# Gate and up weights read in 4 MB transfers, 32 KB per partition, into two neighbouring places of a weight ring

## The chip, the cores and the metric

The kernel runs on one core of a Trainium2 chip. The metric is device microseconds of one execution, median over several. The kernel is written engine by engine: TensorE (PE), VectorE (DVE), ScalarE (ACT), GpSimd (POOL) and SyncE (SP) each have their own program, and they meet only in semaphores. SP and POOL both issue DMA transfers; the 16 DMA engines of the core carry them all.

## The reference

One layer of a hybrid decoder on 320 tokens (256 of a prompt, 64 sampled), everything in float32. Two recurrent branches are merged, projected by `w_o` and added to the input; then a mixture of 32 experts follows, four per token. Cut to what matters:

```python
logits = x2d @ w_router + b_router
top_v, top_e = lax.top_k(logits, TOP_K)            # 4 of 32
gates = softmax(top_v)
def expert(x, e):                                  # d_model 1024, d_ff 1024
    gu = x @ w_gate_up[e] + b_gate_up[e]           # 1024 x 2048: 8 MB
    gate, up = minimum(gu[:, :D_FF], 7), clip(gu[:, D_FF:], -7, 7)
    return ((up + 1) * gate * sigmoid(1.702 * gate)) @ w_down[e] + b_down[e]   # 1024 x 1024: 4 MB
y = rms(x + sum over the four experts of gate * expert(x, e)) * norm_f_w
```

The experts' weights are 32 x 12 MB, 402.7 million bytes, and each byte is used once.

## The kernel before

**Up to the experts.** The mixing part takes about 370 us of the run; its weight panels go through slots 0 to 4 of the ring below (`MIX = 5`), and the four pieces of `w_o` into slots 8 to 11. Then come the product with `w_o`, the norm, the router and the placing of tokens. On PE this is one row of instructions; ahead of the transposes at L1095 (`bgu`) PE waits for `s_late`, a semaphore that six loads issued by POOL raise (L577 to L582: the norm weights broadcast to all partitions) together with two earlier ones. The expert stage begins on PE at the first `gate_up`.

**The ring.** `ring` has 16 slots of 8 KB per partition. For the experts two neighbouring slots make a place (`chunk(p)`, 16 KB per partition, 2 MB), so there are eight places. An expert has six chunks of 2 MB: `c` = 0 to 3 are rows of `w_gate_up`, 256 each (a partition holds two whole neighbouring rows, one run of 16 KB in memory), and `c` = 4, 5 are 512 rows of `w_down` each (four rows of 4 KB per partition, again one run of 16 KB). Chunk `c` of expert `e` has the number `g = 6 e + c` and goes into place `g % 8`. Each place has two semaphores: `e_full[p]`, which the transfer raises by 16, and `e_free[p]`, which PE raises by one when it has read the place.

**SP** first issues eight chunks by hand (`load(g, e)`): 3, 1, 2, 0 as ring slots come free from the mixing panels, 6 and 7 (the first two of expert 1), and, behind the last product with `w_o` (`wo11`), 4 and 5. From `g = 8` on it goes through the chunks in order: wait for the place, issue. SP stands still at each such wait, so transfers are issued in the order of `g`.

**PE** handles two experts in a round (`pair`). `gate_up` reads the four gate/up chunks in order, waiting for each; both halves of the gate and up rows of the 64 token slots come out in two PSUM banks. Then DVE and ACT make the activation while PE does the scatter of the expert before, or the gather of the ones to come, and `down_chunk` reads the two down chunks. The loop runs 8 times over four experts.

Of the kernel before, what the change touches and what calls it, by code (L numbers as in the profile page):

```python
# [51 lines left out]
PIECES = RING // 2  # L52
# [71 lines left out]
def build(nc, x_prompt, x_sample, state_gdn, state_gdn_conv, state_gla, norm1_w, w_in, conv_w, a_log, dt_bias,  # L124
# [3 lines left out]
    with ExitStack() as ctx:  # L128
# [275 lines left out]

        def expert_chunk(e, c):

            w, r, i = (w_gate_up, 256 * c, 2) if c < GU else (w_down, 512 * (c - GU), 4)
            rows_of = w[0][bass.ds(e, 1), r:r + 128 * i, :]
            return rows_of.rearrange("e (p i) n -> p (e i n)", i=i)

# [6 lines left out]
        def piece(e, c):  # L417

            g = CHUNKS * e + c
            return g % PIECES, g // PIECES  # L420

        block = ctx.enter_context(nc.Block())


        @block.sync
        def _(sp):
            for s in range(2):
                sp.dma_start(x_tm[:, s, :], x_prompt[0, 128 * s:128 * s + 128, :]).then_inc(s_x[s], 16)
            sp.dma_start(x_tm[0:64, 2, :], x_sample.rearrange("b t d -> (b t) d")).then_inc(s_x[2], 16)
            sp.dma_start(rows[0:8, :], norm1_w[0].rearrange("(k p) -> k p", p=128)).then_inc(s_rows, 16)  # L430
            sp.dma_start(rows[8:56, :], conv_w[0].rearrange("j (t p) -> (j t) p", p=128)).then_inc(s_rows, 16)
            sp.dma_start(rows[56:57, :], gdn_norm_w).then_inc(s_rows, 16)
            sp.dma_start(rows[57:58, :], gla_norm_w).then_inc(s_rows, 16)
            sp.dma_start(rows[58:60, :], gla_gk_b[0].rearrange("(k p) -> k p", p=128)).then_inc(s_rows, 16)
            sp.dma_start(rows[60:68, :], norm2_w[0].rearrange("(k p) -> k p", p=128)).then_inc(s_rows, 16)
            sp.dma_start(cst_rows, state_gdn_conv[0].rearrange("b w c -> (b w) c")).then_inc(s_cst, 16)
            for i in range(MIX):
                n = panels[i].shape[1]
                sp.dma_start(slot(i).rearrange("p (k n) -> p k n", k=n), panels[i]).then_inc(wfull[i], 16)
                if i == 0:  # L440
                    sp.dma_start(w_small[:, :, 0:8], win(C_AB, 8)).then_inc(s_small, 16)
                    sp.dma_start(w_small[:, :, 8:24], win(C_LR, 16)).then_inc(s_small, 16)
                    sp.dma_start(gk_up[:, :], gla_gk_up[0]).then_inc(s_small, 16)
                    sp.dma_start(hb[:, 0:4], dt_bias.to_broadcast([128, 4])).then_inc(s_misc, 16)
                    sp.dma_start(hb[:, 4:8], a_log.to_broadcast([128, 4])).then_inc(s_misc, 16)
            sp.dma_start(Sg[:, :, :], state_gdn[0].rearrange("b h d e -> d (b h) e")).then_inc(s_state, 16)
            sp.dma_start(Sl[:, :, :], state_gla[0].rearrange("b h d e -> (b h d) e")
                         .rearrange("(n p) e -> p n e", p=128)).then_inc(s_state, 16)
            sp.dma_start(wr[:, :, :], w_router[0].rearrange("(k p) e -> p k e", p=128)).then_inc(s_misc, 16)
            sp.dma_start(brt[:, :], b_router.to_broadcast([128, EXPERTS])).then_inc(s_misc, 16)  # L450
            for i in range(MIX, MIX_PANELS):

                full(sp, last_use[i - MIX])
                n = panels[i].shape[1]
                sp.dma_start(slot(i % MIX).rearrange("p (k n) -> p k n", k=n), panels[i]).then_inc(wfull[i % MIX], 16)
            sp.wait_ge(o_ready, 2)
            full(sp, f"gss{HEADS - 1}1")
            for k in range(WO):
                src = w_o[0][256 * k:256 * k + 256, :].rearrange("(k p) n -> p k n", p=128)
                sp.dma_start(wo_slot(k).rearrange("p (k n) -> p k n", k=2), src).then_inc(wfull[MIX + k], 16)  # L460

            def load(g, e):
                p = g % PIECES
                sp.dma_start(chunk(p), expert_chunk(e, g % CHUNKS)).then_inc(e_full[p], 16)

            load(3, 0)
            for i in range(MIX_PANELS - MIX, MIX_PANELS):
                full(sp, last_use[i])
                if i % MIX in (3, 4, 0):
                    load({3: 1, 4: 2, 0: 0}[i % MIX], 0)  # L470
            sp.wait_ge(out_sem, 16 * 6)
            load(6, 1)
            load(7, 1)
            full(sp, "wo11")
            load(4, 0)
            load(5, 0)
            for g in range(PIECES, 4 * CHUNKS):
                sp.wait_ge(e_free[g % PIECES], g // PIECES)
                load(g, g // CHUNKS)

            def load_quad(i, first):
                for g in range(4 * CHUNKS):
                    sp.wait_ge(e_free[g % PIECES], i * USES + g // PIECES)
                    load(g, first + g // CHUNKS)

            with sp.Fori(1, QUADS) as i:
                load_quad(i, i * 4)
            sp.wait_ge(cnt_ready, 1)
            its = sp.value_load(nit[0:1, 0:1], min_val=QUADS, max_val=QUADS * ROUNDS)
            with sp.If(its > QUADS):  # L490
                with sp.Fori(QUADS, its) as i:
                    load_quad(i, (i % QUADS) * 4)
            sp.wait_ge(fin_dve, 1)
            sp.dma_start(y_prompt[0, 0:128, :], x_tm[:, 0, :]).then_inc(y_out, 16)
            sp.wait_ge(fin_dve, 2)
            for f in range(2):
                sp.dma_start(y_sample.rearrange("b t d -> (b t) d")[:, 512 * f:512 * f + 512],
                             xs[64 * f:64 * f + 64, :]).then_inc(y_out, 16)
            sp.wait_ge(fin_dve, 3)
            sp.dma_start(y_prompt[0, 128:256, :], x_tm[:, 1, :]).then_inc(y_out, 16)  # L500

            sp.wait_ge(out_sem, 16 * 6)
            sp.wait_ge(y_out, 64)
# [3 lines left out]
        def _(pool):  # L507
# [27 lines left out]
            for g in range(2, 4):  # L535
# [14 lines left out]
            step(pool.memset(gb_rows[0:64], 0.0), consts)  # L550


            pool.dma_start(n2p[:, :].rearrange("p (k i) -> p k i", i=2), norm2_w[0].rearrange("(k p i) -> p k i", p=128, i=2)
                           ).then_inc(s_n2p, 16)
            freed(pool, "tail2")
            pool.dma_start(conv_p[0, 0], tail_tm[0:3, :]).then_inc(out_sem, 16)
# [34 lines left out]
        def _(pe):  # L591
# [458 lines left out]
            def first_tokens(s, f):  # L1050

                o = p3(bank[f], 4, 2 * SLOTS)
                pe.wait_ge(first_ready, TILE_ORDER.index(s) + 1)
                for k in range(4):
                    c = 256 * (k // 2) + k % 2
                    if s < 2:
                        lhs, rhs = x_tm[:, s, 512 * f + c:512 * f + c + 255:2], Psel[:, s, :]
                    else:
                        u = slice(64 * f, 64 * f + 64)
                        lhs, rhs = xs[u, c:c + 255:2], Psel[u, 2, :]  # L1060
                    mm = pe.matmul(o[:, k, :], lhs, rhs, start=(s == TILE_ORDER[0] and k == 0),
                                   stop=(s == TILE_ORDER[-1]), skip_group_check=True)
                return mm
# [10 lines left out]
            def turn_tokens(f):  # L1074

                o = p3(bank[f], 4, 2 * SLOTS)
                for k in range(4):
                    c = 512 * f + 256 * (k // 2) + k % 2
                    mm = pe.transpose(o[:, k, :], xr[:, c:c + 255:2], ident[:, :])  # L1079
                mm.then_inc(xt_full[f], 1)  # L1080

            o = take("wo2")
# [74 lines left out]
            def gate_up(x, e, i):  # L1157

                for k in range(KD):
                    p, u = piece(e, k // 2)  # L1160
                    if k % 2 == 0:
                        pe.wait_ge(e_full[p], i * (16 * USES) + (16 * u + 16))
                    for q in range(2):
                        mm = halves(bank[PRE[q]], xTe[:, k, SLOTS * x:SLOTS * x + SLOTS],
                                    chunk(p)[:, 2048 * (k % 2) + FF * q:2048 * (k % 2) + FF * q + FF], k == 0, k == KD - 1)
                    if k % 2:
                        mm.then_inc(e_free[p], 1)
# [7 lines left out]
            def down_chunk(x, e, i, c):  # L1175

                p, u = piece(e, c)
                pe.wait_ge(e_full[p], i * (16 * USES) + (16 * u + 16))
                for j in range(4):
                    mm = halves(bank[DN[x]], hm[x][:, j, c - GU, :], chunk(p)[:, D * j:D * j + D], c == GU and j == 0,  # L1180
                                c == CHUNKS - 1 and j == 3)
                mm.then_inc(e_free[p], 1)
# [854 lines left out]
```

## Time and profile before

| | |
|---|---|
| median of 3 runs | 1367.11 us (1364.9 to 1369.3) |
| the profiled execution | 1367.33 us |
| its span, first to last instruction | 1365.6 us |
| PE busy | 1290.9 us, 95% of the span |
| read from memory | 442.30 MB, 328 GB/s over the span |
| experts' stage | from 434 us on; 425 to 430 GB/s from 444 us to 1331 us |

The span and the time of the profiled execution differ by 1.7 us. PE's busy share counts instructions that overlap and can't be read as a share of its peak; a better reading is where it waits and for what. GB/s is what all 16 DMA engines moved. A transfer appears in the trace as packets on an engine; here one packet is one partition's run, 16 KB for the experts' weights.

### The profile page before, as it was taken

How to read it: one execution, taken by the hardware profiler on the slowest of the kernel's cores; microseconds unless marked ns; L12 is line 12 of the kernel's file. 1: busy time of each engine (PE TensorE's matmuls, PEld its weight loads, DVE VectorE, ACT ScalarE, POOL GpSimd, SP SyncE). 2: the span in 40 equal slices, each digit the busy share in tenths (PEclk: the TensorE clock that was granted, in tenths of full speed). 3: DMA queues.
4: the chain of work that ended last, by engine and by line, in shares of the span. 5: the costliest groups of instructions: out<-in, count | busy, mean ns of one | idle time of the engine just before them, and what ended most of it. 6: DMA issues, size and time to landing. Idle time of an engine off the chain costs nothing.

```text
span 1365.6 us, 15570 instructions
## 1 busy us (share of the span) xinstructions
PE 1290.9 (95%) x5889; PEld 613.5 (45%) x5889; DVE 437.3 (32%) x814; ACT 287.0 (21%) x527; POOL 33.6 (2%) x73
## 2 busy tenths in 40 slices
PE   7999989989989999999999999999999999999996
PEld 5777678746645333333333333333333333333332
DVE  3536565274115231223212322122321212322123
ACT  2375552130022011111110211101111010111103
POOL 6000000001000000000000000000000000000000
PEclk9999989999999999999999999999999999999999
DMA  9622300226584999999999999999999999999993
GB/s 270 182 76 84 94 31 2 62 70 229 221 327 179 425 427 428 427 429 429 429 429 428 429 429 429 429 428 429 428 429 429 428 429 428 429 430 427 429 428 155
DMA packets 61885, 447.76 MB, mean 328 GB/s; under 512 B 7637, under 2 KB 30249, under 8 KB 37276
## 3 DMA queue, kind: packets, MB, share of 16 engines
q1 hardware_dynamic: 59836, 440.34, 78.4%
q0 software_dynamic: 2016, 6.99, 1.5%
q8 instruction: 20, 0.33, 0.1%
q14 instruction: 13, 0.11, 0.0%
HBM read 442.30 MB, written 5.02 MB: 328 GB/s over the span
## 4 chain that ended last, share of the span: by engine, by line
PE 65%; DMA 26%; DVE 6%; ACT 1%; issue 1%; POOL 0%; DVEq 0%; SPq 0%; ACTq 0%
PE bank L668 31%; DMA ring<-in_w_gate_up_dram 24%; PE bank L617 14%; PE bank L1072 5%; DMA xbuf<-in_norm_f_w_dram 2%; PE bank L1079 2%; PE bank L1172 1%; PE bank L871 1%; PE bank L682 1%; PE bank L1006 1%; PE bank L883 1%; PE bank L879 1%; PE bank L1151 1%; DVE qkgb L1987 1%; PE bank L1144 0%
## 5 line engine op out<-in xcount | busy, mean ns | idle before, releaser
L668 PE MATMUL bank<-ring,zgb 128*64 128x512 f32 x2560 | 562.0, 594 | 36.1 <-DMA ring<-in_w_gate_up_dram 27.7
L668 PEld LDWEIGHTS bank<-ring,zgb 128*64 128x64 f32 x2560 | 181.4, 137 | 413.4 <-issue 344.0
L1978 DVE COPY zgb<-bank 128x512 f32<-128x512 f32 x32 | 22.1, 692 | 614.5 <-PE bank L668 614.5
L617 PE MATMUL bank<-hTb,ring 128*128 128x320 f32 x640 | 179.2, 438 | 1.3 <-DVE hTb L1574 1.3
L617 PEld LDWEIGHTS bank<-hTb,ring 128*128 128x128 f32 x640 | 121.7, 192 | 53.7 <-issue 4.6
L668 PE MATMUL bank<-ring,oABb 128*64 128x512 f32 x512 | 116.9, 598 | 0.0
L1504 ACT COPY zgb<-bank 128x512 f32<-128x512 f32 x32 | 18.7, 586 | 419.4 <-PE bank L668 419.4
L1514 ACT COPY hTb<-bank 64x512 f32<-64x512 f32 x64 | 37.1, 579 | 197.6 <-PE bank L668 196.6
L1072 PE MATMUL bank<-h2b,oABb 128*128 128x512 f32 (+1 forms) x192 | 78.3, 609 | 0.0
L1151 PE MATMUL bank<-hTb 128*128 128x512 f32 x136 | 68.2, 606 | 0.0
L1951 DVE TENSOR_TENSOR xbuf<-xbuf,bank 128x512 f32<-128x512 f32 x85 | 58.4, 687 | 20.6 <-PE bank L668 11.2
L668 PEld LDWEIGHTS bank<-ring,oABb 128*64 128x64 f32 x512 | 33.9, 136 | 58.7 <-issue 54.8
L1172 PEld LDWEIGHTS bank<-ident,zgb 128*128 128x128 f32 x256 | 39.1, 204 | 35.1 <-ACT zgb L1504 19.9
L1987 DVE TENSOR_TENSOR qkgb<-bank,masks 128x512 f32<-128x512 f32 x64 | 44.3, 692 | 27.8 <-PE bank L1172 19.4
L1172 PE MATMUL bank<-ident,zgb 128*128 128x128 f32 x256 | 42.3, 288 | 0.0
L617 PE MATMUL bank<-oABb,ring 128*128 128x320 f32 x128 | 38.9, 460 | 2.0 <-DVE oABb L1825 2.0
L1072 PEld LDWEIGHTS bank<-h2b,oABb 128*128 128x128 f32 (+1 forms) x192 | 27.0, 190 | 28.3 <-issue 28.3
L617 PEld LDWEIGHTS bank<-oABb,ring 128*128 128x128 f32 x128 | 25.6, 203 | 16.4 <-issue 4.9
L1151 PEld LDWEIGHTS bank<-hTb 128*128 128x128 f32 x136 | 22.3, 193 | 22.9 <-issue 22.9
L1491 ACT COPY h2b<-bank 128x512 f32<-128x512 f32 x32 | 18.7, 585 | 61.3 <-PE bank L1072 61.3
L1495 ACT COPY zgb<-bank 128x512 f32<-128x512 f32 x32 | 18.7, 585 | 59.1 <-PE bank L1079 58.4
L1508 ACT ACTIVATE qkgb<-qkgb 128x512 f32<-128x512 f32 x32 | 20.2, 630 | 42.7 <-DVE qkgb L1989 42.2
(384 smaller groups left out, 952.4 us busy)
## 6 DMA issues: line engine op xcount, KB each, us to landing
ring<-in_w_gate_up_dram SPq DMA_DIRECT2D x128, 2048.0 KB, 30.5
ring<-in_w_down_dram SPq DMA_DIRECT2D x64, 2048.0 KB, 34.9
ring<-in_w_in_dram SPq DMA_DIRECT2D x22, 1024.0 KB, 5.4
ring<-in_w_o_dram SPq DMA_DIRECT2D x4, 1024.0 KB, 12.5
ring<-in_w_up_a_dram SPq DMA_DIRECT2D x2, 1024.0 KB, 5.0
ring<-in_w_up_b_dram SPq DMA_DIRECT2D x2, 1024.0 KB, 5.0
out_dram<-ring POOLq DMA_DIRECT2D x1, 2048.0 KB, 14.2
xbuf<-in_x_prompt_dram SPq DMA_DIRECT2D x2, 512.0 KB, 4.0
```

Source lines behind the costliest of these rows:

```text
L617: mm = pe.matmul(o[0:m, 0:TOK], w[:, k, c0:c0 + m], rhs[:, k, :], start=(k == 0), stop=(k == kk - 1))
L668: mm = pe.matmul(o[64 * f:64 * f + 64, 0:width], lhs, w[f] if isinstance(w, list) else w[:, width * f:width * f + width], start=start, sto ...
L1072: return pe.matmul(o[:, :], lhs, rhs, start=(s == TILE_ORDER[0]), stop=(s == TILE_ORDER[-1]))
L1079: mm = pe.transpose(o[:, k, :], xr[:, c:c + 255:2], ident[:, :])
L1151: mm = pe.matmul(bank[SC[j]][:, :], GTs[:, TILE_0[s]:TILE_0[s] + 128], y_sl[:, 512 * f:512 * f + 512], start=True, stop=True)
L1172: mm = pe.transpose(bank[FMB[q]][:, 128 * j:128 * j + 128], pre[:, q, j:512:4], ident[:, :])
L1491: link(nc.scalar.copy(xr[:, 512 * f:512 * f + 512], bank[7 - f][:, :]), xr_done, done)
L1508: link(A(sbuf_[:, :, :, :], gbuf[:, :, :, :], ACT.Sigmoid, scale=ALPHA), sg_ready, n * 2 + (x + 1))
L1514: ins = nc.scalar.copy(y_sl[SLOTS * x:SLOTS * x + SLOTS, 512 * f:512 * f + 512], bank[DN[x]][64 * f:64 * f + 64, :])
L1951: link(TTo(v, v, bank[SC[j]][:, :], ALU.add), acc_done, n * 5 + i)
L1978: link(V.tensor_copy(pre[:, 1, :], bank[PRE[1]][:, :]), pre_done[1], n * 2 + (x + 1))
L1987: inner(TTo(dst[:, :, :, :], src, bias, ALU.add))
```

## The change

A transfer of gate/up weights now takes 512 rows, four per partition: a run of 32 KB, 4 MB in all, into two neighbouring places. `load` is called for chunks 1 and 3 of an expert after both places are free (chunks 0 and 2 only wait) and issues for the pair; it raises `e_full` of the first place alone. PE waits once per pair (`landed` works out the count), and still gives the two places back one by one. Since a partition holds rows 4p to 4p+3 now instead of 2p and 2p+1, the gathered tokens are taken with a step of 4 instead of 2 (`first_tokens`, `turn_tokens`), and so is the norm weight `n2p`. The down chunks are as they were. In the hand-written start, the separate loads of chunks 3 and 1 are gone, and that of chunk 7.

```diff
-            w, r, i = (w_gate_up, 256 * c, 2) if c < GU else (w_down, 512 * (c - GU), 4)
+            w, r, i = (w_gate_up, 256 * c, 4) if c < GU else (w_down, 512 * (c - GU), 4)
...
+        def landed(eng, e, i, c):
+
+            g = CHUNKS * e + c
+            starts = [q for q in range(4 * CHUNKS) if q % PIECES == g % PIECES and q % CHUNKS not in (1, 3)]
+            eng.wait_ge(e_full[g % PIECES], i * (16 * len(starts)) + 16 * (starts.index(g) + 1))
...
-                p = g % PIECES
-                sp.dma_start(chunk(p), expert_chunk(e, g % CHUNKS)).then_inc(e_full[p], 16)
-
-            load(3, 0)
+                p, c = g % PIECES, g % CHUNKS
+                n = 8192 if c < GU else 4096
+                sp.dma_start(ring[:, 4096 * p:4096 * p + n], expert_chunk(e, c)).then_inc(e_full[p], 16)
+
             for i in range(MIX_PANELS - MIX, MIX_PANELS):
                 full(sp, last_use[i])
-                if i % MIX in (3, 4, 0):
-                    load({3: 1, 4: 2, 0: 0}[i % MIX], 0)
+                if i % MIX in (4, 0):
+                    load({4: 2, 0: 0}[i % MIX], 0)
             sp.wait_ge(out_sem, 16 * 6)
             load(6, 1)
-            load(7, 1)
             full(sp, "wo11")
             load(4, 0)
             load(5, 0)
             for g in range(PIECES, 4 * CHUNKS):
                 sp.wait_ge(e_free[g % PIECES], g // PIECES)
-                load(g, g // CHUNKS)
+                if g % CHUNKS not in (0, 2):
+                    load(g - (g % CHUNKS < GU), g // CHUNKS)
...
-                    c = 512 * f + 256 * (k // 2) + k % 2
-                    mm = pe.transpose(o[:, k, :], xr[:, c:c + 255:2], ident[:, :])
+                    mm = pe.transpose(o[:, k, :], xr[:, 512 * f + k:512 * f + 512:4], ident[:, :])
...
                     p, u = piece(e, k // 2)
-                    if k % 2 == 0:
-                        pe.wait_ge(e_full[p], i * (16 * USES) + (16 * u + 16))
+                    if k % 4 == 0:
+                        landed(pe, e, i, k // 2)
```

SP's program just ahead of the experts' stage, before: `pfull` are the semaphores of the mixing part's last products, `outputs` that of the stored states, `piece_free` that of a place.

```order
L460 DMA ring<-in_w_o_dram 128x2x1024 x3
L464 DMA ring<-in_w_gate_up_dram 128x4096
L464 DMA ring<-in_w_gate_up_dram 128x4096 [waits pfull6,pfull5,pfull4]
L464 DMA ring<-in_w_gate_up_dram 128x4096 [waits pfull3]
L464 DMA ring<-in_w_gate_up_dram 128x4096 [waits pfull4]
L464 DMA ring<-in_w_gate_up_dram 128x4096 [waits outputs]
L464 DMA ring<-in_w_gate_up_dram 128x4096
L464 DMA ring<-in_w_down_dram 128x4096 [waits pfull7]
L464 DMA ring<-in_w_down_dram 128x4096
L464 DMA ring<-in_w_gate_up_dram 128x4096 [waits piece_free0]
L464 DMA ring<-in_w_gate_up_dram 128x4096 [waits piece_free1]
```

The same place of SP's program now (`w_o` stands at L466, `load` at L471):

```order
L466 DMA ring<-in_w_o_dram 128x2x1024 x3
L471 DMA ring<-in_w_gate_up_dram 128x8192 [waits pfull6,pfull3,pfull5,pfull4]
L471 DMA ring<-in_w_gate_up_dram 128x8192 [waits pfull4]
L471 DMA ring<-in_w_gate_up_dram 128x8192 [waits outputs]
L471 DMA ring<-in_w_down_dram 128x4096 [waits pfull7]
L471 DMA ring<-in_w_down_dram 128x4096
L471 DMA ring<-in_w_gate_up_dram 128x8192 [waits piece_free1,piece_free0]
```

The transfer that followed `w_o` without a wait (chunk 3) is no longer there; its 2 MB now come with the first transfer behind the mixing part's last product, and the first refill of the ring waits for two places instead of one.

PE's program at the first `gate_up` of a round, before (`piece_full` is raised by a transfer):

```order
L668 MATMUL bank<-ring,zgb 64x512 [waits piece_full0]
L668 MATMUL bank<-ring,zgb 64x512 x7
L668 MATMUL bank<-ring,zgb 64x512 [waits piece_full1]
L668 MATMUL bank<-ring,zgb 64x512 x7
L668 MATMUL bank<-ring,zgb 64x512 [waits piece_full2]
L668 MATMUL bank<-ring,zgb 64x512 x7
L668 MATMUL bank<-ring,zgb 64x512 [waits piece_full3]
```

And now (the matmuls stand at L675):

```order
L675 MATMUL bank<-ring,zgb 64x512 [waits piece_full0]
L675 MATMUL bank<-ring,zgb 64x512 x15
L675 MATMUL bank<-ring,zgb 64x512 [waits piece_full2]
L675 MATMUL bank<-ring,zgb 64x512 x15
```

Four waits of PE have become two, each for 4 MB. (In this listing one row is a pair of the instructions that the profile counts, so x16 in a profile row is one place.)

## Rows read from the trace of the kernel before

**Rows 1.** The page: GB/s in 40 slices of the span, 34.1 us each.

```profile
GB/s 270 182 76 84 94 31 2 62 70 229 221 327 179 425 427 428 427 429 429 429 429 428 429 429 429 429 428 429 428 429 429 428 429 428 429 430 427 429 428 155
```

**Rows 2.** Chain that ended last, 1270 to 1366: start us, us, what.

```profile
1299.63 33.40 DMA ring<-in_w_gate_up_dram
```

**Rows 3.** Timeline of PE, 1297 to 1355: start, us, instructions [idle before <- releaser].

```profile
1328.18 3.65 PE L668 MATMUL bank<-ring,zgb 128*64 128x512 f32 x16 [0.82 <-DMA ring<-in_w_gate_up_dram]
1333.08 3.65 PE L668 MATMUL bank<-ring,zgb 128*64 128x512 f32 x16 [1.24 <-DMA ring<-in_w_gate_up_dram]
```

**Rows 4.** Chain that ended last, 420 to 700: the same place of two rounds.

```profile
509.29 20.82 PE bank L668 x96
...
564.47 20.82 PE bank L668 x96
```

**Rows 5.** Landing, issue to last byte, of ring transfers issued at 373.8, 437.7, 1307.5.

```profile
DMA to landing us min/median/max: 32.4/32.4/32.4
...
DMA to landing us min/median/max: 7.8/7.8/7.8
...
DMA to landing us min/median/max: 35.2/35.2/35.2
```

**Rows 6.** Chain that ended last, 371 to 434.5.

```profile
374.54 25.25 DMA xbuf<-in_norm_f_w_dram
...
399.83 1.13 PE bank L1095 x4
```

**Rows 7.** Timeline of PE, 430 to 462.

```profile
433.99 13.95 PE L668 MATMUL bank<-ring,zgb 128*64 128x512 f32 x64 [0.91 <-DVE zgb L1934]
```

**Rows 8.** Timeline of SP's issues, 330 to 480: first issue, length of the row, transfers.

```profile
340.54 33.81 SPq L464 DMA_DIRECT2D ring<-in_w_gate_up_dram  x6
...
437.68 3.76 SPq L464 DMA_DIRECT2D ring<-in_w_gate_up_dram  x2
...
457.69 10.63 SPq L464 DMA_DIRECT2D ring<-in_w_gate_up_dram  x4
```

**Rows 9.** DMA queues, 345 to 351: packets, MB, share of 16 engines.

```profile
q1 hardware_dynamic: 652, 2.49, 102.5%
```

**Rows 10.** DMA queues, 600 to 1300 (q1 is SP's, q0 POOL's).

```profile
q1 hardware_dynamic: 20597, 299.98, 100.7%
```

**Rows 11.** DMA queues, 371 to 407.

```profile
q1 hardware_dynamic: 720, 10.49, 75.9%
q0 software_dynamic: 480, 1.57, 11.3%
```

**Rows 12.** DMA queues, 371 to 376.

```profile
q1 hardware_dynamic: 65, 1.06, 63.9%
```

**Rows 13.** DMA queues, 376 to 389.

```profile
q1 hardware_dynamic: 302, 4.42, 81.2%
q0 software_dynamic: 287, 1.05, 20.2%
```

**Rows 14.** DMA queues, 389 to 399.8.

```profile
q1 hardware_dynamic: 228, 3.23, 86.9%
q0 software_dynamic: 193, 0.52, 13.4%
```

**Rows 15.** DMA queues, 323 to 333.

```profile
q0 software_dynamic: 729, 2.92, 76.4%
q1 hardware_dynamic: 788, 0.79, 25.8%
```

**Rows 16.** Instructions of lines 1079 and 1172: duration ns min/median/max, first and last start.

```profile
L1079 PE MATMUL bank<-ident,h2b x128: 281/283/385, 480.8 to 1347.5; 128*128 128x128 f32 x128
...
L1172 PE MATMUL bank<-ident,zgb x256: 272/284/387, 448.8 to 1339.5; 128*128 128x128 f32 x128
```

**Rows 17.** Timeline of PE, 300 to 312.

```profile
304.31 1.13 PE L980 MATMUL bank<-ring,xbuf 32*128 32x512 f32 x4 [2.36 <-DVE ring L1803]
```

**Rows 18.** Busy time by engine in one stretch, then PEclk, DMA share, GB/s.

```profile
305.80:309.20 3.40, 3.40 (x8) 1.51 (x5) 3.19 (x7) 0.00 (x0) 0.00 (x0) 0.50 0.01 2
```

More of the change, by code:

```diff
@@ L483, in load_quad @@
                     sp.wait_ge(e_free[g % PIECES], i * USES + g // PIECES)
-                    load(g, first + g // CHUNKS)
+                    if g % CHUNKS not in (0, 2):
+                        load(g - (g % CHUNKS < GU), first + g // CHUNKS)
             with sp.Fori(1, QUADS) as i:
@@ L550, in _ @@
             step(pool.memset(gb_rows[0:64], 0.0), consts)
-            pool.dma_start(n2p[:, :].rearrange("p (k i) -> p k i", i=2), norm2_w[0].rearrange("(k p i) -> p k i", p=128, i=2)
+            pool.dma_start(n2p[:, :].rearrange("p (k i) -> p k i", i=4), norm2_w[0].rearrange("(k p i) -> p k i", p=128, i=4)
                            ).then_inc(s_n2p, 16)
@@ L1056, in first_tokens @@
                     if s < 2:
-                        lhs, rhs = x_tm[:, s, 512 * f + c:512 * f + c + 255:2], Psel[:, s, :]
+                        lhs, rhs = x_tm[:, s, 512 * f + k:512 * f + 512:4], Psel[:, s, :]
                     else:
                         u = slice(64 * f, 64 * f + 64)
-                        lhs, rhs = xs[u, c:c + 255:2], Psel[u, 2, :]
+                        lhs, rhs = xs[u, k:512:4], Psel[u, 2, :]
                     mm = pe.matmul(o[:, k, :], lhs, rhs, start=(s == TILE_ORDER[0] and k == 0),
@@ L1177, in down_chunk @@
                 p, u = piece(e, c)
-                pe.wait_ge(e_full[p], i * (16 * USES) + (16 * u + 16))
+                landed(pe, e, i, c)
                 for j in range(4):
```

## The prediction

> **What bounds the kernel now.** I read first what the DMA moves over the span. From slice 14 on, that is from 444 us to 1331 us, it moves 425 to 430 GB/s without a gap, and ahead of that far less [rows 1]. So there are two parts: a stretch of 900 us in which the expert weights stream, and what comes before it. Then the chain of waits: its last long piece is a ring transfer that was issued at 1299.6 us and landed 33.4 us later [rows 2], and PE starts on it at once, after waits of 0.8 to 1.2 us [rows 3]. From the first refill of the ring, issued at 437.7 and landed 7.8 us later, to the last, issued at 1307.5 and landed after 35.2 us [rows 5], 183 further places land in 1342.7 - 445.5 = 897.2 us, 4.90 us each. A transfer that lands after 33 us has thus stood behind six others: the queue is full. PE would be a little faster than this. Early on, while it still lives on places filled ahead, two experts take it 564.47 - 509.29 = 55.18 us [rows 4]; their twelve places take the DMA 12 x 4.90 = 58.8 us. PE has 3.6 us to spare per two experts, and the stream is the bound. Its start matters as much as its rate: the stream can't begin before PE gives back a first place, at 437.7 us, one place after PE's first `gate_up` at 433.99 [rows 7, 8]. And what sets 433.99? The chain there goes through a load of POOL's, 25.25 us long, the last of the norm weights; PE stands at L1095 until it has landed and starts again at 399.83 [rows 6].
>
> **The change, part by part.** The sum is made against the profiled execution, 1367.33 us, 0.2 us above the median of the runs shown.
>
> *Longer packets.* Between 345 and 351 us SP's queue moves 4 KB packets: 2.49 MB are 608 of them in 102.5% of 16 x 6 us, 161.8 ns each [rows 9]. In the stream, 299.98 MB are 18309 packets of 16 KB in 100.7% of 16 x 700 us, 616.0 ns each [rows 10]. The twelve KB between them cost 37.85 ns each, so 10.4 ns of each packet don't depend on its length. The ring brings 122 gate/up places after the start, 61 pairs; a pair has 8 packets per engine fewer. 61 x 8 x 10.4 ns = **-5.1 us**. It is nothing if a run of 32 KB goes as two packets.
>
> *First refill.* The first transfer into the ring now needs two places back. PE gives them back 3.43 us apart (two issues of SP take 3.76 us, the last of them 0.33) [rows 8]. The stream starts **+3.4 us** later.
>
> *A seam.* The next pair, chunks 0 and 1 of expert 2, goes at 461.1 instead of 457.7 [rows 8]. What is ahead of it: the first pair, issued at 441.1, would land at 441.1 + 7.8 + 4.9 = 453.8, two down chunks at 463.6. A transfer into an idle queue lands 2.9 us later than its 4.9 us of data; this one is issued 2.5 us before the queue runs dry: **+0.4 us**. Later pairs come earlier against the queue, since PE gains 3.6 us per two experts.
>
> *Pairs given back late.* In the stream every pair is issued 3.4 us after its first place is free. That costs nothing, for the queue holds six transfers ahead [rows 2]; without that cover it would be 61 x 3.4 = 209 us. PE's wait for 4 MB instead of 2 is hidden too, in the 3.6 us that PE has to spare, but not at the end.
>
> *The last pair.* Chunks 2 and 3 of expert 31 land at the same distance from the end of the stream as chunk 3 did, but PE had read chunk 2 by then [rows 3]. Now it reads both afterwards: **+3.4 us**, and everything behind (activation, down, scatter, norm, output) moves with it.
>
> *The norm loads.* This is the largest term, and it lies before the stream. Chunk 3 was issued at 340.54 [rows 8], in idle time, long before POOL's loads. Now its 2 MB stand with the others behind the mixing part, beside the six loads for which PE waits at L1095. How do the two queues share an engine? From 323 to 333 us POOL's queue moves 2.92 MB in packets of 4 KB, 713 of them, and SP's 0.79 MB in packets of 1 KB, 771 [rows 15]. From 376 to 389 us POOL's moves 1.05 MB, 256 packets, and SP's 4.42 MB, now in packets of 16 KB, 270 [rows 13]. Bytes stand once 4:1 and once 1:4, packets both times 1:1. So an engine takes one packet from each queue in turn, whatever its size, and a packet of POOL's will wait for 32 KB instead of 16. Per engine POOL has 384 / 16 = 24 packets and SP had 640 / 16 = 40 [rows 11]; now SP has 12.6 MB, 24 packets of 32 KB, of which two are gone when POOL's first packet comes, at 376 (65 small ones, 4 per engine, until then [rows 12]). The first 16 turns took 13.0 us [rows 13] and get 16 x 0.61 = 9.8 us longer. The last eight took 10.8 us, with 3.23 MB = 12.3 of SP's packets per engine [rows 14]: 12.3 x 0.616 + 8 x 0.16 = 8.9 us and 1.9 us of pauses. Now SP has only 22 - 16 = 6 left: 6 x 1.22 + 8 x 0.16 + 1.9 = 10.5 us. Together **+9.5 us**, the norm weights land at about 409.3. PE's row behind L1095 is nearly without gaps up to 433.99, so the expert stage moves by the whole of it. Bounds: nothing, if POOL's turn doesn't get longer; and 11.3 us, when POOL's last packet comes behind all of SP's (SP's last transfer landed at 373.8 + 32.4 = 406.2 [rows 5], with 2 MB more at 411.1).
>
> The Trainium skill, page "DMA: Bandwidth & Descriptors", section "Queues, rings and completion order", also has an engine go round its queues packet by packet, but says that a packet is typically 9 to 17 descriptors long, where the trace shows single runs alternate. By that rule SP's 24 runs would pass in two or three turns and POOL's loads would end last: that is the 11.3 us, and the sum below would be 13.4 instead of 11.6.
>
> *The rest.* A step of 4 instead of 2 in the operands costs nothing: transposes with a step of 2 take 283 ns, with 4 they take 284 [rows 16].
>
> Sum: -5.1 + 3.4 + 0.4 + 3.4 + 9.5 = +11.6 us, 1367.3 + 11.6 = **1379 us**.
>
> **The rivals.**
> *A run of 32 KB goes as two packets of 16 KB.* Then POOL's turns stay as they are and the saving is nothing: 3.4 + 0.4 + 3.4 = +7.2, 1374.5 us. The rows have no packet above 16 KB that could exclude it.
> *POOL's loads aren't held up, the saving holds.* +7.2 - 5.1 = +2.1, 1369.4 us, no measurable change. It needs an engine that shares by bytes, which rows 13 and 15 both speak against.
> *Faster: a price per transfer goes with the transfers.* In the ring 61 transfers fewer are issued. If each seam between transfers cost the stream something, that is saved; it decides from (11.6 + 4.1) / 61 = 0.26 us per seam, and 0.3 us would give 1367.3 + 11.6 - 18.3 = 1360.6 us. Against it: a place lands every 4.90 us, and its 8 packets per engine alone take 8 x 0.616 = 4.93, so no time is left for a seam.
> The same page of the Trainium skill, section "Anatomy of one DMA — SWDGE (gpsimd) path", fits 2.0 us of fixed cost per transfer besides its bytes. Were that paid at every seam, 61 x 2.0 = 122 us would go and the time be about 1257; the 4.90 us per place show it hidden behind the queue.
> *Slower still: PE's clock falls in the longer waits.* PE's waits, up to 1.2 us each now, gather into one per expert, the longer of them over 2 us. At 304.3 us PE had idled 2.36 us, and from 305.8 to 309.2 the granted clock was 0.50, the lower of its two levels, 1.2 of 2.4 GHz [rows 17, 18]; that costs half of 3.4 us, 1.7 us. Twice per two experts makes 55.2 + 3.4 = 58.6 us, still just the stream's 58.8, so only the tail pays, +1.7, 1380.7 us; if PE becomes the bound in part, up to 1386.
>
> **How the numbers follow.** Chances: the sum as it stands 0.64, two packets 0.11, the clock 0.07, POOL unhindered 0.10, faster 0.08. About 0.3%, 4.1 us, is what a measurement of this kernel tells from no change; so the first three are slower, 0.82 together, the fourth is no change and the fifth faster. The range must leave out no more than 0.2: it reaches from 1371, which leaves out the last two, to 1386, which takes in the upper bound of the norm loads (1380.8) and the clock; the lower one is the fourth case.
>
> **What would show it.** Right: PE's wait at L1095 ends near 409 instead of 399.8, its first `gate_up` starts near 443.5; the first refill is issued 7.1 us after that; packets of 32 KB near 1222 ns; the stream from first issue to last landing near 900 us instead of 905; the last wait of PE is followed by 32 matmuls of L675 instead of 16. Wrong: POOL's loads landing by 400, which takes off 9.5 us; packets that are no cheaper, or dearer, per byte (1% of the stream is 9 us); gaps in the stream, where a pair waits for its second place with an empty queue.

## The result, and the profile after

| | before | changed |
|---|---|---|
| median | 1366.71 us (1364.9 to 1369.3, 4 runs) | 1388.09 us (1384.02 to 1393.19, 4 runs) |
| profiled execution, its span | 1367.33, 1365.6 us | 1384.02, 1382.3 us |
| ratio of the times | | 1.0154, 95% interval 1.0132 to 1.0176 |

The changed kernel is slower, as forecast, but by 21.4 us and not by 11.6: the time lies above the range that ended at 1386. Run again beside other kernels, it took 1385.31 us (1383.17 to 1386.92, 4 runs; ratio 1.0133, 1.0114 to 1.0152). The profiled execution was the fastest of its four, so the traces account for 16.7 us between the two spans; what put the other three 2.6 to 9.2 us above it is in no trace.

The first view after is the chain of waits of the changed kernel, from the norm loads to the first `gate_up` of the experts (start us, us, what). It answers to [rows 6].

```profile
372.85 34.59 DMA xbuf<-in_norm_f_w_dram
...
407.48 1.13 PE bank L1102 x4
...
448.14 1.07 PE bank L675 x3
```

The load that took 25.25 us takes 34.59, though it starts 1.7 us earlier. PE starts again at 407.48 instead of 399.83. But from there to the first `gate_up` it now needs 448.14 - 407.48 = 40.66 us, where it needed 433.99 - 399.83 = 34.16. Nothing in the sum stood for these 6.5 us. 0.7 of them lie ahead of `first_tokens` (the rows of L1068 below): its first row starts 432.43 - 407.48 = 24.95 us behind the restart, where before it was 424.05 - 399.83 = 24.22. Behind the longer wait the granted clock stays at 0.50 until 413.9, 6.4 us long; before, it was 0.52 for the first 5.2 us. The other 5.8 us lie between that row and the first `gate_up`.

What PE does in between is in its timeline, changed kernel (start, us, instructions, idle before and what ended it):

```profile
430.84 0.97 PE L1034 MATMUL bank<-wr,hTb 128*128 128x32 f32 x8
...
432.43 3.28 PE L1068 MATMUL bank<-oABb,xbuf 64*128 64x128 f32 x16
435.64 1.92 PE L1034 MATMUL bank<-wr,hTb 128*128 128x32 f32 x8
437.37 4.00 PE L1068 MATMUL bank<-oABb,xbuf 128*128 128x128 f32 x16
...
443.10 4.10 PE L1068 MATMUL bank<-oABb,xbuf 128*128 128x128 f32 x16 [0.61 <-DVE oABb L1887]
447.00 0.85 PE L1141 MATMUL bank<-ident,vTM 128*32 128x128 f32 x3
448.14 13.95 PE L675 MATMUL bank<-ring,zgb 128*64 128x512 f32 x64 [0.29 <-DVE zgb L1941]
```

And the same place in the timeline of the kernel before (L1061 there is L1068 here, L1027 is L1034):

```profile
424.05 1.79 PE L1061 MATMUL bank<-oABb,xbuf 64*128 64x128 f32 x16
425.77 1.08 PE L1027 MATMUL bank<-wr,hTb 128*128 128x32 f32 x8
426.69 2.13 PE L1061 MATMUL bank<-oABb,xbuf 128*128 128x128 f32 x16
...
430.55 2.15 PE L1061 MATMUL bank<-oABb,xbuf 128*128 128x128 f32 x16 [0.62 <-DVE oABb L1880]
432.54 0.54 PE L1134 MATMUL bank<-ident,vTM 128*32 128x128 f32 x3
```

The three rows of `first_tokens`, whose weights the change reads with a step of 4 instead of 2, grow from 1.79 + 2.13 + 2.15 = 6.07 us to 3.28 + 4.00 + 4.10 = 11.38. The unchanged L1034 between them takes 1.92 instead of 1.08, though the same eight took 0.97 at 430.84. That is the clock. The busy time by engine in three stretches of the changed kernel shows it (PE, PEld, DVE, ACT, POOL, then the granted clock, DMA share, GB/s):

```profile
413.90:434.40 20.50, 20.46 (x87) 12.24 (x86) 6.64 (x23) 5.97 (x16) 0.00 (x0) 1.00 0.12 35
434.40:441.20 6.80, 6.80 (x31) 6.51 (x29) 1.93 (x9) 1.54 (x2) 1.33 (x2) 0.50 1.00 426
...
444.60:448.00 3.40, 3.25 (x14) 2.58 (x13) 1.41 (x3) 0.06 (x1) 0.00 (x0) 0.50 0.00 0
```

The first row of `first_tokens` had begun at 432.43 and was already slow while the clock was at its upper level; the fall to the lower one, 1.2 GHz, came 2 us later. What stretched is the weight load, as the instructions of the one line show, in the changed kernel:

```profile
L1068 PEld LDWEIGHTS bank<-oABb,xbuf x48: 305/329/333, 432.4 to 446.6; 128*128 128x128 f32 x32, 64*128 64x128 f32 x16
```

and in the kernel before (ns, min/median/max):

```profile
L1061 PEld LDWEIGHTS bank<-oABb,xbuf x48: 190/196/198, 424.1 to 432.3; 128*128 128x128 f32 x32, 64*128 64x128 f32 x16
```

A load takes 329 ns instead of 196, and that at either level of the clock: 326 in median until 434.3, 330 from there to 441.

Behind the first `gate_up`, SP's issues of the changed kernel answer to [rows 8]:

```profile
455.31 0.33 SPq L471 DMA_DIRECT2D ring<-in_w_gate_up_dram  x1
458.70 3.76 SPq L471 DMA_DIRECT2D ring<-in_w_down_dram  x2
...
475.32 7.20 SPq L471 DMA_DIRECT2D ring<-in_w_gate_up_dram  x2
```

The first refill goes 455.31 - 448.14 = 7.17 us behind the first `gate_up`, not 3.69. The last transfer of the ring is issued at 1324.3, and lands after:

```profile
DMA to landing us min/median/max: 31.7/31.7/31.7
```

So the stream lasts from 455.3 to 1356.0, 900.7 us, where it lasted 905.1. At its end PE's timeline shows, in place of the two rows of 16 matmuls in [rows 3], one of 32:

```profile
1346.31 7.09 PE L675 MATMUL bank<-ring,zgb 128*64 128x512 f32 x32 [2.15 <-DMA ring<-in_w_gate_up_dram]
```

The whole difference, step by step, from the two profiled executions:

| stretch | before, us | changed | difference | forecast |
|---|---|---|---|---|
| start of the span to the last norm load | 374.54 | 372.85 | -1.7 | 0 |
| that load to PE's restart | 25.29 | 34.63 | +9.3 | +9.5 |
| restart to the first `gate_up` | 34.16 | 40.66 | **+6.5** | **0** |
| first `gate_up` to the first refill | 3.69 | 7.17 | +3.5 | +3.4 |
| first refill to the ring's last landing | 905.1 | 900.7 | -4.4 | -5.1 + 0.4 |
| last gate/up landing to the end of the span | 32.6 | 36.0 | +3.4 | +3.4 |

The ring's last landing, a down chunk, follows the last of gate/up by some 9.8 us in both, so the last two rows overlap by that much twice. The differences add up to 16.6 of the 16.7 us. The -1.7 lies ahead of every edit that acts there and is taken as variation between runs.

### The profile page after: what moved, and what is told of

Its sections match the earlier page's. It is cut to its first block, busy times and chain, and to the rows that moved or that the text cites. A ratio compares the mean times of both kernels' runs of the same rounds, so it can differ in the third digit from the quotient of the medians.

```text
span 1382.3 us, 15464 instructions
## 1 busy us (share of the span) xinstructions
PE 1300.0 (94%) x5889; PEld 620.3 (45%) x5889; DVE 437.4 (32%) x814; ACT 287.3 (21%) x527; POOL 33.7 (2%) x73
## 4 chain that ended last, share of the span: by engine, by line
PE 65%; DMA 28%; DVE 5%; issue 1%; ACT 1%; POOL 0%; SPq 0%; DVEq 0%; ACTq 0%
PE bank L675 31%; DMA ring<-in_w_gate_up_dram 25%; PE bank L624 14%; PE bank L1079 5%; DMA xbuf<-in_norm_f_w_dram 3%; PE bank L1086 2%; PE bank L1179 1%; PE bank L878 1%; PE bank L1013 1%; PE bank L689 1%; PE bank L890 1%; PE bank L1068 1%; PE bank L886 1%; PE bank L1158 1%; PE bank L666 1%
## 5 line engine op out<-in xcount | busy, mean ns | idle before, releaser
L675 PE MATMUL bank<-ring,zgb 128*64 128x512 f32 x2560 | 565.1, 598 | 34.7 <-DMA ring<-in_w_gate_up_dram 27.0
L675 PEld LDWEIGHTS bank<-ring,zgb 128*64 128x64 f32 x2560 | 183.3, 138 | 413.4 <-issue 358.0
L675 PE MATMUL bank<-ring,oABb 128*64 128x512 f32 x512 | 116.9, 598 | 0.0
L1079 PE MATMUL bank<-h2b,oABb 128*128 128x512 f32 (+1 forms) x192 | 78.3, 609 | 0.0
L675 PEld LDWEIGHTS bank<-ring,oABb 128*64 128x64 f32 x512 | 33.9, 136 | 58.7 <-issue 54.8
L1179 PEld LDWEIGHTS bank<-ident,zgb 128*128 128x128 f32 x256 | 39.1, 205 | 35.1 <-ACT zgb L1511 19.9
L1079 PEld LDWEIGHTS bank<-h2b,oABb 128*128 128x128 f32 (+1 forms) x192 | 27.0, 190 | 28.3 <-issue 28.3
L1013 PE MATMUL bank<-ring,h2b 128*128 128x512 f32 x64 | 29.7, 612 | 0.0
## 6 DMA issues: line engine op xcount, KB each, us to landing
out_dram<-ring POOLq DMA_DIRECT2D x1, 2048.0 KB, 14.4
```

The lines of the kernel that those rows point to most:

```text
L675: mm = pe.matmul(o[64 * f:64 * f + 64, 0:width], lhs, w[f] if isinstance(w, list) else w[:, width * f:width * f + width], start=start, sto ...
L1013: mm = pe.matmul(o[:, :], merged[:, s, k, :], wo_slot(k // 2)[:, c:c + 512], start=(k == 0), stop=(k == KD - 1))
L1079: return pe.matmul(o[:, :], lhs, rhs, start=(s == TILE_ORDER[0]), stop=(s == TILE_ORDER[-1]))
L1179: mm = pe.transpose(bank[FMB[q]][:, 128 * j:128 * j + 128], pre[:, q, j:512:4], ident[:, :])
```

## The experiments

The theory after the result: the norm loads (9.3 us), the step of 4 in `first_tokens` (most of the 6.5 us), and a ring that pays 3.5 + 3.4 us at its ends for 4.4 us of longer packets. The rivals: the longer idle time at L1102 lowers PE's clock, and that, not the step, stretches `first_tokens`; and it is the 61 transfers fewer, not the longer packets, that shorten the stream. Of the ten kernels four ran side by side, then four, then two, each time beside the kernel before.

**The changed kernel again.** No edit.

> The changed kernel once more, beside the others. If its 21 us are a sum of fixed steps, it comes out 16 to 22 us above the kernel before, and its trace shows the same steps: PE's wait at L1102 of about 14.5 us, the 48 matmuls of L1068 at about 233 ns from one to the next, first refill 7.2 us after the first gate_up, stream 900 us. If the spread of its runs (1384 to 1393) comes from something that differs from run to run, one of these steps differs in this trace.

Measured: 1385.31 us, as told above. Its trace repeats the steps: PE waits 14.4 us at L1102, restart to `gate_up` 39.1 us, refill 7.17 us behind it, stream 900.7 us, 36.1 us at the end. From restart to `gate_up` it is 1.5 us shorter than in the first trace, and that is the clock: the 0.7 us behind the wait are not there, and the fall under `first_tokens` lasted 3.4 us (clock 0.51) instead of 6.8.

**4 MB transfers with two runs of 16 KB.** The ring's transfers, waits and places stay as changed; only the length of a run, and with it all steps of 4, go back.

```diff
             rows_of = w[0][bass.ds(e, 1), r:r + 128 * i, :]
+            if c < GU:
+                return rows_of.rearrange("e (h p i) n -> p (e h) (i n)", h=2, i=2)
...
+                dst = ring[:, 4096 * p:4096 * p + n]
+                if c < GU:
+                    dst = dst.rearrange("p (h n) -> p h n", h=2)
```

> Still 4 MB transfers into two places, but each partition gets two runs of 16 KB (rows 2p, 2p+1 of either half), so packets are as before and the operand steps are 2 again. Theory (packet length holds up the norm loads, the step of 4 slows the token matmuls, the pairs cost 3.5 us at the first refill and 3.4 us at the end): norm loads land as before, PE's wait about 5 us, L1068 at 117 ns, no saving in the stream: 1367 + 6.9 = 1374 us. Rival (4 MB transfers and the waits for two places are themselves the cost): it stays near 1388 us.

Measured: 1376.83 us (1374.25 to 1379.16, 6 runs; ratio 1.0064, 1.0048 to 1.0080). The list of PE's waits has the norm loads at

```profile
PE bank L1107 <- DMA xbuf<-in_norm_f_w_dram: 5.7, 1, 5.7
```

instead of 14.5 in the changed kernel and 5.2 before. So 2 MB more behind the mixing part are harmless; it is the 32 KB run that holds the norm loads up. The stream takes 905.9 us, the time of before: without longer packets nothing is saved, although 61 transfers fewer are issued. The refill (+3.5) is as in the changed kernel. So is the end, but for the clock: at 1340.5 to 1343.9, in the tail, it was 0.50, and the end took 37.7 us instead of 36.0. PE's row from restart to `gate_up` took 35.6 us, 1.4 more than before; the clock was 0.62 from 400.8 to 411. The execution traced is the slowest of the six, 1379.16 us; which of this is in the 2.8 us of the median above the expectation isn't shown.

**The ring's loads behind the norm loads.** In the changed kernel, SP waits until all of POOL's norm loads have landed before it issues the three gate/up transfers.

```diff
                 full(sp, last_use[i])
+                if i % MIX == 4:
+                    sp.wait_ge(s_late, 128)
```

> The changed kernel, but SP waits for the norm loads before it issues the first three 4 MB transfers. Theory: the norm loads, alone on the engines, land at about 381 us, PE doesn't wait at L1102; against the changed kernel 9.3 + 5.2 us of waiting and some 2.5 us of halved clock are gone, about 1371 us, while the token matmuls of L1069 still stand 233 ns apart. Rival (PE's long idle time at L1102 sets the slow clock behind it, and that alone slows the token matmuls): they return to 117 ns, another 6 us, about 1365 us.

Measured: 1368.95 us (1366.22 to 1370.88, 12 runs; ratio 1.0008, 0.9998 to 1.0019). The norm loads land at 380.84 and PE doesn't wait for them. Its timeline:

```profile
388.08 7.11 PE L1015 MATMUL bank<-ring,h2b 128*128 128x512 f32 x16
395.03 0.63 PE L1104 MATMUL bank<-ident,h2b 128*128 128x128 f32 x4
...
417.00 3.27 PE L1070 MATMUL bank<-oABb,xbuf 64*128 64x128 f32 x16
420.20 1.91 PE L1036 MATMUL bank<-wr,hTb 128*128 128x32 f32 x8
421.93 4.03 PE L1070 MATMUL bank<-oABb,xbuf 128*128 128x128 f32 x16
```

and its busy time and clock by stretch:

```profile
412.00:417.00 5.00, 4.96 (x22) 2.77 (x21) 0.69 (x1) 2.62 (x5) 0.00 (x0) 1.00 0.27 52
417.00:419.00 2.00, 2.00 (x13) 2.00 (x13) 0.85 (x2) 0.47 (x3) 0.00 (x0) 0.99 0.64 238
419.00:425.80 6.80, 6.80 (x31) 6.47 (x29) 1.93 (x9) 1.58 (x2) 1.33 (x2) 0.50 1.00 426
```

The row of `first_tokens` is as long as in the changed kernel, with no wait at L1104 and the clock at its upper level when it begins; then the clock falls all the same. The rival that makes it a consequence of idle time is out. The line that the expectation names is one off: `first_tokens` is L1070 here.

**A step of 2 in `first_tokens`.** In the changed kernel, that operand alone goes back to its old columns.

```diff
-                        lhs, rhs = x_tm[:, s, 512 * f + k:512 * f + 512:4], Psel[:, s, :]
+                        lhs, rhs = x_tm[:, s, 512 * f + c:512 * f + c + 255:2], Psel[:, s, :]
```

(and the same for `xs` below it).

> The changed kernel, with the step of the token operand of first_tokens put back to 2; the first gathered tokens then stand in an order that doesn't fit the weights, which changes values, not work. Theory (the step of 4 in the weight load doubles the time of these 48 matmuls, and the clock falls under them): they go back to 117 ns, 5.6 + 0.9 us less, 6.5 us under the changed kernel, about 1381.5 us, with the wait at L1102 unchanged. Rival (the clock after the long idle does it): they stay near 233 ns and the time near 1388 us.

Measured: 1380.33 us (1379.84 to 1381.84, 5 runs; ratio 1.0096, 1.0080 to 1.0112), 5.0 us below the changed kernel beside it. The line's instructions:

```profile
L1068 PEld LDWEIGHTS bank<-oABb,xbuf x48: 191/196/198, 433.1 to 441.3; 128*128 128x128 f32 x32, 64*128 64x128 f32 x16
```

Restart to `gate_up` takes 34.8 us, nearly the 34.16 of before, and the wait at L1102 stays (14.7 us). What is left is the sum as it was forecast, and the time is 1.3 us above its 1379.

**A step of 4 in the kernel before.** The reverse edit, alone.

> The kernel before with nothing changed but the step of the token operand of first_tokens, 4 instead of 2; the gathered tokens then don't fit the order of the weights, which changes values, not work. Theory: 48 matmuls at 233 ns instead of 117 from one to the next, and the clock falls under them: 5.6 to 7 us over the kernel before, about 1373.5 us. Rival (the step is free, as the transposes said): 1367.5 us.

Measured: 1376.12 us (1370.12 to 1377.38, 7 runs; ratio 1.0048, 1.0029 to 1.0066), 9.4 us more than before. Its trace:

```profile
L1061 PEld LDWEIGHTS bank<-oABb,xbuf x48: 305/330/333, 426.3 to 440.6; 128*128 128x128 f32 x32, 64*128 64x128 f32 x16
```

Restart to `gate_up` takes 41.4 us (+7.2), and the clock falls too, from 428.7 to 435.5 and once more from 438.9 to 445.8. The second fall reaches into the first `gate_up`, so the first refill comes 5.45 us behind it and not 3.69. Together 9.0 us; the expected time stood 6.8 us above before. The seven runs lie far apart: the two fastest, 1370.1 and 1370.8 us, had a mean granted clock of 0.986, nearly that of before, the other five, 1372.9 to 1377.4, one of 0.981 to 0.983, and the trace is of the slowest. That fits a step that costs more the longer the clock falls behind it; with one trace of the seven it isn't shown.

**The same wait in the kernel before.** The same line, with `i % MIX == 3`: the ring's loads behind chunk 3 wait for the norm loads.

> The kernel before with one wait more: SP lets the norm loads land before it issues chunk 1 and what follows. Theory (packets of 16 KB already hold the norm loads up, by some 19 us, of which PE waits 5.2): they land at about 381 us, PE's wait at L1095 and the halved clock behind it are gone, 7 to 8 us under the kernel before, about 1360 us. Rival (the later weights then come too late for the first experts, or the time lies in the stream alone): no gain, 1367 us or more.

Measured: 1358.98 us (1357.75 to 1361.82, 6 runs; ratio 0.9944, 0.9931 to 0.9957), 7.7 us less than before. The norm loads land at 378.42, PE goes through without a wait, and restart to `gate_up` takes 31.9 us at a clock of 1.00, where before its first 5.2 us ran at 0.52 behind the wait. The delay of the norm loads was thus no child of the change; the change made an old one longer.

**Both ends in halves.** In the changed kernel, chunks 2 and 3 of every second expert, the first refill and the last pair among them, go as two transfers of 2 MB in the same rows, with 16 KB runs; each has a semaphore.

```diff
+                if g // CHUNKS in split and g % CHUNKS in (2, 3):
+                    load_half(g, g // CHUNKS)
...
+                    if k == 6 and e in split:
+                        pe.wait_ge(split[e], i * 16 + 16)
```

> The changed kernel, with chunks 2 and 3 of every second expert, the first refill and the last pair among them, loaded as two transfers of 2 MB again (16 KB of each run). Theory (a pair costs one place of PE at the first refill and one at the end): the first refill goes 3.7 us after the first gate_up instead of 7.2, and PE reads 16 matmuls after the last landing of gate/up instead of 32; 16 pairs lose their saving, 1.2 us: 5.7 us under the changed kernel, about 1379.5 us. Rival (both ends are hidden): 1386 us.

Measured: 1385.17 us (1383.62 to 1386.07, 4 runs; ratio 1.0134, 1.0119 to 1.0149), no gain: the expectation of 1379.5 failed. The first refill did come 3.69 us behind `gate_up`, and the end is 33.6 us instead of 36.0. But the stream took 906.1 us. SP's issues:

```profile
451.90 3.76 SPq L479 DMA_DIRECT2D ring<-in_w_gate_up_dram  x2
458.77 3.76 SPq L473 DMA_DIRECT2D ring<-in_w_down_dram  x2
...
475.39 7.19 SPq L473 DMA_DIRECT2D ring<-in_w_gate_up_dram  x2
```

The second down chunk, issued at 462.2, took the first of these landing times, and the pair behind it, issued at 475.4, the second:

```profile
DMA to landing us min/median/max: 13.0/13.0/13.0
...
DMA to landing us min/median/max: 12.2/12.2/12.2
```

The queue ran dry at 475.2, just as the pair of expert 2 was issued; it landed 12.3 us behind its predecessor, where in the changed kernel the same pair followed in 9.7. So 2.6 of the 3.5 us that the earlier refill had won were waited out one pair later. A quarter of the pairs also move in 16 KB runs again, which at about 11 ns a packet (below) is 61 / 4 x 8 x 0.011 = 1.3 us. The remaining 1.5 of the 5.4 us by which the stream is longer isn't put to one place. What was shown is that the wait moved from the first refill to the next pair.

**The halves behind the norm loads.** The changed kernel with both: the halves, and the ring's loads behind the norm loads.

> Both mends of the changed kernel together, halves at the ends and SP's wait for the norm loads. If the parts add up: 1368.95 - 5.7 = 1363.2 us, under the kernel before, though the token matmuls keep their step of 4. If one hides the other, 1367 to 1369 us.

Measured: 1367.89 us (1366.19 to 1370.35, 12 runs; ratio 1.0007, 0.9998 to 1.0016), not to be told from 1368.95 without the halves, as in the second of the two cases expected. The stream takes 906.0 us again. The first refill comes 5.50 us behind `gate_up` and not 3.69.

**8 KB runs beside the norm loads.** In the kernel before, the five early gate/up loads take rows p and p + 128 into a partition, which makes two runs of 8 KB.

```diff
+                sp.dma_start(chunk(p).rearrange("p (i n) -> p i n", i=2),
+                             rows_of.rearrange("e (i p) n -> p (e i) n", i=2)).then_inc(e_full[p], 16)
```

> The kernel before; only the five transfers that stand beside the norm loads (chunks 1, 2, 0 of expert 0 and 0, 1 of expert 1) take rows p and p + 128 instead of 2p and 2p + 1, so that a run is 8 KB; these five chunks then don't fit the order of the tokens, which changes values, not work. Theory (an engine takes one packet from either queue in turn): a turn gets 0.3 us shorter, 24 turns some 6 to 7 us, the norm loads land near 393 instead of 400, ahead of PE, and its wait of 5.2 us and part of the halved clock behind it go: about 1361 us. Rival (the engines share by bytes, or the 2 MB more in the queue is what delays the loads): they land at 400 as before, 1367 us.

Measured: 1358.03 us (1357.63 to 1361.06, 6 runs; ratio 0.9930, 0.9914 to 0.9946), 10.2 us below before. The DMA queues from 375 to 390 us (packets, MB, share):

```profile
q1 hardware_dynamic: 473, 3.61, 69.8%
q0 software_dynamic: 468, 1.57, 32.3%
```

Nearly one for one again, 3.61 MB in runs of 8 KB against 1.57 MB in runs of 4: some 440 and 384 of them. All 1.57 MB of POOL's pass in these 15 us, the norm loads land at 391.33, and PE, at 393.03, doesn't wait for them.

**Norm loads first and a step of 2.** The changed kernel with both of its large costs taken out, which leaves the ring.

> The changed kernel with SP's wait for the norm loads, and the step of the token operand put back to 2 (gathered tokens that don't fit the order of the weights: other values, the same work). What is left of the change is then the ring alone: longer packets, first refill, last pair. If the parts add up: 1358.98 (the kernel before with the same wait) + 3.5 + 3.5 - 4.4 = 1361.6 us. Rival (the pairs cost the stream or PE more than these ends): 1364 us or more.

Measured: 1362.33 us (1360.88 to 1364.94, 6 runs; ratio 0.9952, 0.9938 to 0.9967). Restart to `gate_up` is 31.9 us, and the clock stays at 1.00 through `first_tokens`; with the step of 4 alone added, in the experiment with the loads behind the norm loads, it fell there, and the time was 1368.95 us, 6.6 more. The stream takes 901.2 us and the refill comes after 7.17. In PE's timeline the last pair reads

```profile
1325.50 8.78 PE L677 MATMUL bank<-ring,zgb 128*64 128x512 f32 x32 [2.13 <-DMA ring<-in_w_gate_up_dram]
```

which is 1.7 us longer than in the changed kernel, because the clock fell just there:

```profile
1326.80:1330.30 3.50, 3.50 (x12) 1.02 (x10) 0.00 (x0) 0.00 (x0) 0.00 (x0) 0.51 1.01 431
```

The kernel before with the same wait took 1358.98: the ring alone costs 3.4 us by these two medians, and 1.8 when each is held against the kernel before that ran beside it (5.9 and 7.7 us below). The terms of the ring had made it 2.1.

## Why the prediction was right in sign and wrong in size

**The step that failed** is the last and shortest one, "A step of 4 instead of 2 in the operands costs nothing". It was read from transposes [rows 16], 284 ns against 283, and carried over to the matmuls of `first_tokens`. Their weight loads take 196 ns with a step of 2 and 329 with 4, shown in both kernels and both ways round (1385.31 to 1380.33 us when it is taken out, 1366.69 to 1376.12 when it is put in). 48 of them lie on the path: they cost between 5.0 and 9.4 us, by how much of the clock's fall that follows hits rows on the path. The sum also let the stage move by the whole of the norm loads' delay and no more; the longer low clock behind the wait added 0.7 us in the first of the two traces of the changed kernel, and nothing in the second. With the 6.5 us of the trace the sum is 1379.0 + 6.5 = 1385.5 us, where the two medians are 1388.1 and 1385.3.

What sets the two kinds apart is not that `first_tokens` has its strided operand as a weight, for the transposes have it there too. At L1134 a tile with 32 columns is transposed, and it is 32 columns that are loaded as weights (128x32), while 128 stream. The same listing has the loads of the lines of rows 16, in the kernel before:

```profile
L1134 PEld LDWEIGHTS bank<-ident,vTM x3: 94/97/106, 432.4 to 432.9; 128*32 128x32 f32 x2, 64*32 64x32 f32 x1
...
L1079 PEld LDWEIGHTS bank<-ident,h2b x128: 195/209/219, 480.8 to 1347.3; 128*128 128x128 f32 x128
...
L1172 PEld LDWEIGHTS bank<-ident,zgb x256: 195/208/220, 448.6 to 1339.4; 128*128 128x128 f32 x128
```

With a step of 2 (L1079) and of 4 (L1172) the loads of transposes take the same time. A transpose has one load, an fp32 matmul of `first_tokens` two (48 for 24). Whether the slow load hangs on that, on the transposing or on something else, no run shows. The rows of L1061 in the trace of before had no step of 4 either; but they show other instructions than those of rows 16, and a bound on the side of a loss was needed there.

The Trainium skill, page "SBUF — State Buffer", section "Door 1: The DMA port swizzle (why `[64,N]` ≈ `[32,N]`)", gives SBUF lines of 16 bytes and asks for at least two hits in a line for full rate. With fp32 a step of 2 gives two hits and a step of 4 one. The loads of 196 and 329 ns in `first_tokens` agree with that, the loads of 209 and 208 ns in the transposes don't. The same passage calls a step of 4 fp32 free, which the transposes bear out and `first_tokens` does not.

**The norm loads**: +9.3 for a forecast +9.5, PE's restart at 407.5 for "near 409", which is the same once the start 1.7 us earlier is taken off. Packets did alternate one for one; from 376 to 389 us the queues of the changed kernel show

```profile
q1 hardware_dynamic: 162, 4.78, 86.4%
q0 software_dynamic: 160, 0.59, 11.4%
```

that is 146 runs of 32 KB and 144 of 4 KB, in a time that had been enough for 256 of POOL's [rows 13]. Runs of 8, 16 and 32 KB on SP's queue gave landings at 391.3, 399.8 and 407.4 us, in the order that turns by packet ask for. Turns of several runs, as the Trainium skill has them (page "DMA: Bandwidth & Descriptors", section "Queues, rings and completion order"), would have made it 11.3 us; this trace, with 146 runs against 144, disagrees.

**Longer packets**: -4.4 for -5.1 + 0.4. From 600 to 1300 us the queue now moves

```profile
q1 hardware_dynamic: 13808, 301.47, 100.4%
```

which is 0.5% more than in [rows 10]. By the packets' records a run of 32 KB took 1217 ns from 600 to 1300 us and 1221 over the whole stream, and two of 16 KB 2 x 614.7, so 9 to 12 ns are saved with each packet fewer, for a forecast 10.4. So a run of 32 KB is one packet, and the first rival is out. The forecast seam of 0.4 us at the pair of expert 2 didn't occur in the changed kernel: the pair was issued at 475.3, 3.1 us before the last transfer ahead of it landed, and landed 9.7 us behind that one. In the halves it did occur. Where the 0.7 us between -5.1 and -4.4 went isn't shown.

**First refill and last pair**: +3.5 and +3.4 for +3.4 each. That pairs are given back late and that PE waits longer cost nothing between: its waits were 0.68 and 2.14 us by turns (at 908 and 937 us), under the 3.6 us that it had to spare.

**The rivals.** A price per transfer went with nothing: with 61 transfers fewer and runs of 16 KB the stream took 905.9 us for 905.1. The clock in the tail did fall in some executions, two of those profiled, and cost the +1.7 us worked out for it; in the changed kernel's own profile it did not. Whether that, or the falls behind `first_tokens`, make the spread of its runs, 1383 to 1393 us, stays open: only one execution of each set has a trace, and the two of the changed kernel are the fastest of theirs.

**The parts by experiment.** The ring alone 1.8 to 3.4 us. The norm loads: the same wait gives the changed kernel 16.4 us and the kernel before 7.7, which leaves 8.7 to the change. The step 5.0 to 9.4, and 6.6 with the norm loads first. Together 15.5 to 21.5, and the two comparisons measured 17.8 and 21.4.

## What to carry to other kernels

A price read from one kind of instruction holds for that kind: where an edit changes how an operand is read, look for a row of the same instruction with the new step, and put a bound on the loss where there is none. Before runs on a full queue are made longer, look at which short loads of another queue must come through beside them; a wait that holds the long ones back until the short ones have landed gave this kernel 7.7 us without the change, more than the longer runs could. A gain at a queue's start is kept only if the next transfers are ready too: 3.5 us earlier here became a dry queue one pair later.

## What the runs showed of the hardware

- Weight loads of the fp32 matmuls of `first_tokens` take 196 ns with a step of 8 bytes and 329 ns with 16; the weight loads of transposes with the same steps take 209 and 208 ns. Why those are spared was not tried.
- The granted clock fell to 0.50 with no idle time of PE ahead: from 412 to 419 us in the experiment with the loads behind the norm loads PE was busy for 6.96 of 7 us, the last 2 of them with slow weight loads, and the next 6.8 us ran at half the clock. With a step of 2 in the same place it stayed at 1.00. That slow weight loads bring the fall is shown by the pair; what the chip goes by is not.
- An engine took one packet from each of two queues in turn at all lengths seen: SP's 1, 8, 16 and 32 KB against 4 KB of POOL's (771 packets against 713, some 440 against 384, 270 against 256, 146 against 144). How long POOL's loads take is therefore set by the other queue's run length, not by its bytes.
- A packet of 16 KB took 614.7 ns and one of 32 KB 1217 to 1221: some 9 to 12 ns of a packet don't depend on its length.
